# Prompt attention: the value products of a step stand behind its second and later turns

## The reference

```
s = einsum('bqhd,bkhd->bhqk', q, k) * SCALE + bias
p = masked_softmax(s, mask)
o = einsum('bhqk,bkhd->bqhd', p, v)
```

## Time and profile before

| what | value |
|---|---|
| median of 3 runs | 1965.08 us |
| the profiled execution's own time | 1964.52 us |
| its span | 1962.8 us |
| PE busy | 1808.4 us (92%) |
| DVE busy | 990.1 us (50%) |
| ACT busy | 740.3 us (38%) |
| POOL busy | 504.7 us (26%) |
| granted PE clock, mean | 0.978 |

### The profile page before, as it was taken

The page is one execution under the profiler, slowest core; times in us unless marked ns, Lnnn a source line. Parts: engine busy times, 40 slices in busy tenths (PEclk is TensorE's granted clock), DMA queues, the critical chain, the costliest instruction groups (busy, mean ns, idle before and its releaser), DMA issues. The chain is left out here.

```text
span 1962.8 us, 31183 instructions
## 1 busy us (share of the span) xinstructions
PE 1808.4 (92%) x11465; PEld 1594.4 (81%) x11465; DVE 990.1 (50%) x1909; ACT 740.3 (38%) x1477; POOL 504.7 (26%) x604
## 2 busy tenths in 40 slices
PE   4999999998878789999997998999999999999996
PEld 4898777998644678888886887999999999976784
DVE  4233421333343777777777542333333333375997
ACT  3234411211322377777777332111112111243453
POOL 5020032421444532222212101211112221133523
PEclk9799999999999899999998998999999999999999
DMA  8544343356967973333312121111111111164543
GB/s 185 80 107 156 119 154 117 114 165 214 351 233 266 205 206 71 66 65 65 93 38 79 66 88 42 52 53 43 43 43 43 43 53 53 46 229 146 202 136 142
DMA packets 169903, 229.30 MB, mean 117 GB/s; under 512 B 45018, under 2 KB 113477, under 8 KB 169665
## 3 DMA queue, kind: packets, MB, share of 16 engines
q1 hardware_dynamic: 143298, 152.77, 26.1%
q0 software_dynamic: 24400, 72.81, 13.1%
q10 hardware_dynamic: 2080, 2.10, 0.4%
HBM read 192.65 MB, written 40.24 MB: 119 GB/s over the span
## 5 line engine op out<-in xcount | busy, mean ns | idle before, releaser
L121 PE MATMUL gate_acc<-o_T_hi,w_gate_split_hi 128*128 128x352 f32 x528 | 171.5, 325 | 2.3 <-ACTq L2817 2.3
L121 PE MATMUL up_acc<-o_T_hi,w_up_split_hi 128*128 128x352 f32 x528 | 170.6, 323 | 0.7 <-DVEq L2881 0.7
L122 PE MATMUL gate_acc<-o_T_lo,w_gate_split_hi 128*128 128x352 f32 x528 | 170.3, 323 | 0.0
L123 PE MATMUL gate_acc<-o_T_hi,w_gate_split_lo 128*128 128x352 f32 x528 | 170.2, 322 | 0.0
L122 PE MATMUL up_acc<-o_T_lo,w_up_split_hi 128*128 128x352 f32 x528 | 169.2, 321 | 0.0
L123 PE MATMUL up_acc<-o_T_hi,w_up_split_lo 128*128 128x352 f32 x528 | 169.1, 320 | 0.0
L2305 ACT ACTIVATE pa_scores<-pa_scores,pa_neg_max 128x128 f32<-128x128 f32 (+1 forms) x192 | 143.5, 747 | 16.6 <-DVE pa_neg_max L2345 13.2
L2393 DVE TENSOR_TENSOR pa_probs_T_lo<-pa_t,pa_probs_T_hi 128x512 fp32r<-128x512 f32 (+2 forms) x240 | 124.0, 533 | 29.3 <-ACT pa_probs_T_hi L2320 27.1
L2939 POOL TENSOR_TENSOR w_gate_split_lo<-w_gate,w_gate_split_hi 128x1024 fp32r<-128x1024 f32 x21 | 50.4, 2400 | 341.5 <-ACT w_gate_split_hi L2827 341.5
L2320 ACT ACTIVATE pa_probs_T_hi<-pa_t 128x512 fp32r<-128x512 f32 (+2 forms) x240 | 110.8, 476 | 67.8 <-PE pa_t L2244 64.8
L2244 PE MATMUL pa_t<-ident,pa_scores 128*128 128x128 f32 x688 | 115.7, 275 | 20.6 <-DVE pa_probs_T_lo L2393 19.8
(11 more groups left out here) (456 smaller groups left out, 4828.5 us busy)
## 6 DMA issues: line engine op xcount, KB each, us to landing
w_down_raw<-in_w_down SPq DMA_DIRECT2D x59, 512.0 KB, 4.5
fox_k_pages<-in_cache_fox_kv SPq DMA_DIRECT2D x64, 256.0 KB, 5.7
w_rows<-in_cache_fox_kv POOLq DMA_DIRECT2D x48, 256.0 KB, 4.8
w_gate<-in_w_gu SPq DMA_DIRECT2D x22, 512.0 KB, 3.9
w_up<-in_w_gu SPq DMA_DIRECT2D x22, 512.0 KB, 3.9
w_rows<-in_w_in SPq DMA_DIRECT2D x5, 2048.0 KB, 8.5
sel_pages<-in_cache_nsa_kv POOLq DMA_DIRECT2D x64, 128.0 KB, 5.5
pa_k_fox<-scratch_kf_d POOLq DMA_DIRECT2D x32, 256.0 KB, 6.8
```

Of the source, the lines that this page charges most:

```text
L121: pe.matmul(out, a[0][at], b[0][bt], start=start, stop=False)
L122: pe.matmul(out, a[0][at], b[1][bt], start=False, stop=False)
L123: return pe.matmul(out, a[1][at], b[0][bt], start=False, stop=stop)
```

## The change

Of a step's turns the first has no value products behind it any more. The products of the pair are shared out behind the second and later turns: with two turns in the step (A and B) all of them stand behind the second, with four turns (C and D) a third stands behind each of the other three. The order of the products, the number of them and the order of everything else stay as they are. The wait that stands ahead of the first product moves with it.

```diff
                     for n in now[side]:
                         turn(n)
-                        if live:
-                            values(p, x / rounds, (x + 1) / rounds)
+                        if live and x:
+                            values(p, (x - 1) / (rounds - 1), x / (rounds - 1))
                         x += 1
                 if live and not x:
                     values(p, 0, 1)
```

## The result

The changed kernel takes 1947.41 us (median of 4 runs, 1942.97 to 1949.22), beside 1964.7 us before (4 runs, 1959.79 to 1965.45). The ratio is 0.9912, with a 95% interval of 0.9896 to 0.9928, so 14 to 20 us are gained. Forecast were 1951 us and 14 us of gain, range 1946 to 1959. Single runs of one kernel scatter: over all that follows, those of the kernel before lie between 1956.71 and 1967.58 us (0.6%), and twelve runs of one experiment span 0.8%. The traces are steadier than that: the same piece of a job repeats within 0.02 us in nearly all jobs of a trace. So parts of the gain are read from them.

The account below looks back on a forecast made before the run. PE was taken to lead one piece of each job and DVE the other, so shortening PE's piece shortens the job. Gains 8.8 + 2.5 + 2.6 = 13.9 us, rounded to 14, gave 1951 us; range 1946 to 1959.

Parts of the forecast that it names:

- R1: Rival: the job is paced by something other than PE in step A; no change, 1962.5 to 1965 us; chance 0.09.
- Step A, sel and win jobs, 0.55 us: Scores, back and turn cover the 0.65 us stall, less 0.10 us at `back`; 16 steps, 8.8 us.
- Step A, fox jobs, 0.36 us: The stall before the first value product, 0.36 us, goes in seven fox jobs: 2.5 us.
- Step C, 0.12 us a job: Scores of t7 come 0.12 us earlier, shrinking DVE's idle time; up to 2.9 us over 24 jobs, 2.6 taken.
- Step B, 0: The pair's 4 products go behind t3's turn; no wait stands at either place, DVE leads soon after: 0.
- Step D, 0: 12 products shared 4, 4, 4; the 0.91 us wait for DVE stays, turns t6b and t7a come earlier: 0.
- The stages behind keep their lengths, the clock stays: Later stages keep their lengths; the change makes no wait longer, so the granted clock was not expected to fall.
- R4: Rival: PE's granted clock falls to 1.2 GHz for a twentieth of its time; +4 us, 1969 us; chance 0.02.
- R2: Rival: in step A a wait at t1's turn or `back` holds up all products; middling +8 us, 1973; chance 0.05.
- R3: Rival: DVE is also freed in steps B and C and step C's stalls go; some 19 us, 1946; chance 0.05.
- The signs: Step A's 23 product waits go, turns' 19.8 us stay within 3, DVE's 1.24 us goes, PE busy stays 354 us.

Follow-up runs that it names:

- the wait kept: Changed kernel's order, but PE waits for DVE's last subtraction where it did before, behind the first turn: 1957.7 us beside 1961.12 for the kernel before.
- A and B only: Changed kernel with the new order only in two-turn steps, the old order in four-turn steps: 1950.42 us beside 1961.12 for the kernel before.
- C only: Changed kernel with the new order only in step C, the old order elsewhere: single run, 1960.17 us beside 1964.27 for the kernel before.
- late copy: Changed kernel, but in step A ACT copies the value products out behind the copy of t0's turn: 1954.23 us beside 1962.03 for the kernel before.
- products behind the scores: Changed kernel, but two-turn steps put half the products behind the second scores, half behind the second turn; four-turn steps as before: 1948.9 us beside 1961.12.

## Why the prediction was right, step by step

- *PE leads from step D to the next step B, and its stall is paid in full.* Right. The run with the wait kept gives P2 back while all else stays changed. R1 is out.
- *Step A, sel and win jobs, 0.55 us.* Right mechanism, and two errors that partly cancel. The stall was 0.75 us and not 0.65. I compared the first product's start (884.74) with where it should have been. But the row of a product right behind a turn starts early: in the changed kernel two transposes start at 888.04 and the product at 888.18, 0.14 us later and not 0.22. The second product is the sure mark: 888.38 is 0.34 us after 888.04, which is two transposes and one product. In the kernel before the second product of step A stood at

```profile
884.96 0.28 PE L2264 MATMUL pa_o<-pa_probs_T_lo,pa_v_fox 128*128 128x256 f32 x1
```

  and, behind one transpose and one product, should have stood at 883.98 + 0.23 = 884.21: 0.75 us. `back`'s wait was 0.29 us in the run with A and B only, twice the 0.15 of my calculation with ACT unmoved. 0.75 - 0.29 = 0.46, the measured 8.72 to 8.26. ACT did keep its times there: the copy ends 0.73 us behind the start of t0's turn, as in the kernel before (884.71 less 883.98). What I had left out are two small delays. `back` starts 0.79 us behind the turn, 0.06 us after the copy's end, and the turn behind `back` follows at 0.27 us (888.62 to 888.89) and not at 0.21. 0.15 + 0.06 + 0.06 = 0.27 of the 0.29 us. Step D's part makes the copy 0.12 us earlier, where I had taken 0.05, and so the wait 0.17 and the gain 0.58 us. That 0.55 came so near is luck: the stall was 0.10 too small and the wait at `back` 0.07.
- *Step A, fox jobs, 0.36 us.* Mis-sized by the same mark: 0.45 us, and 0.46 in the changed kernel. The one of the seven that I left out (0.47 us in the idle column and not 0.19) gained 0.74.
- *Step C, 0.12 us a job.* Right in the mechanism, and mis-sized: 0.17, 0.16 and 0.08, 3.3 us for the 24 jobs, beside the 2.6 that I took (3.5 in the changed kernel). In a sel job the scores of t7 come 0.16 us earlier (3.98 us behind the bias of t4 before, 3.82 with C only), 0.04 more than the one product; where these come from stays open. That t4b's turn takes over the wait of the products was right: the 8 waits of value products that are not in step A stood in step C of the window jobs, 0.28 us each, and 8 of 0.26 to 0.27 us stand at t4b's turn now.
- *Step B, 0.* Wrong. A gap of 0.1 us in a fox job and 0.03 in the others stood there, too small for the list of idle times, 8 x 0.16 = 1.3 us.
- *Step D, 0.* Wrong in the sum, though its mechanism stood in the prediction (t7b's turn comes one product earlier). I used it for ACT's copy and gave it 0.05 us. It is 0.12 us in sel and win jobs: 16 x 0.12 = 1.9 us beyond A's own.
- *The stages behind keep their lengths, the clock stays.* Right: from the last addition to the span's end it is 899.1 us before and 898.4 now, and the clock is no lower anywhere. R4 is out. R2 did not happen, but the run with the late copy shows that 0.3 us more of lateness would have cost 7 us of the gain. R3 is partly true: DVE's gaps in steps B and C did close, its 0.20 us wholly, but the waits in step C that it wanted gone stay. 1947.41 us lies 0.6 us below the forecast's own range of 1948 to 1955, between it and R3's 1946.
- *The signs.* The 23 waits of step A are gone, the turns' waits stayed (18.5 us), DVE's 1.24 us went, and its entry ahead of t4 grew, to 1.6 us and not 1.2. PE's busy time did not stay at 354 us: it is 348.75, with as many matmuls. No run was made for this.

The sum was 13.9 us and the pieces give 17.3. The difference by terms: B +1.3, D +1.9, C +0.9, fox jobs' step A +0.7, and the other jobs' step A 16 x (0.46 - 0.55) = -1.4, together +3.4. The forecast was short because two steps were set to nothing on the ground that no wait was listed in them.

What stays open: 0.02 us of `back`'s wait, in the run with A and B only as in the changed kernel (0.15 of 0.17 us by the rows), and the 0.04 us of step C.

## What to carry to other kernels

Products that wait for the last result of the step before are best put behind work that does not need it, and the gain is the stall in full only in a stretch that their engine leads; so cut the period into the pieces that each engine leads, and price an edit by the piece in which it stands. Then follow the order of every engine for what comes next: here the next wait (`back` for ACT's copy) took 0.17 to 0.29 of 0.75 us. Once PE was further ahead, `back` one turn later on PE did not take it away, and a new order on ACT did. An edit in one step that hands its result on earlier (step D) is worth something in the next one, even where its own step is not limited by it.

## What the runs showed of the hardware

On PE, the row of the first product behind a pause, and of one behind a turn, is no sure mark of when work went on. The second product's start is: products follow each other at 0.12 us (888.38 back to 888.18 is 0.20, and all after it 0.12), and stalls measured to the second start agree with the pieces to 0.01 us. In a sel job it is 0.75 us, and with the products behind the scores 0.29 us by the second start and 0.46 us off P2. In a fox job it is 0.46 us (second product at 868.61) and 0.45 off P2. By the first start they are 0.10 and 0.09 us short (0.65 and 0.36).

From the end of ACT's copy to the start of the `back` that waits for it, the rows show 0.05 to 0.06 us: 0.73 to 0.79 us behind t0's turn with A and B only, 0.61 to 0.67 in the changed kernel, 0.92 to 0.97 with the product copy late.
